# Second attention with softmax numerators turned by VectorE and value products in eight tiles; inverse sums spread by DMA

## The chip, the cores and the metric

The kernel runs on one core of one Trainium2 chip. The core has a matrix engine (TensorE, PE in the rows), whose weight loads have rows of their own (PEld), and four others: VectorE (DVE), ScalarE (ACT), GpSimd (POOL) and SyncE (SP), which issues most DMA transfers. Each engine works through its own queue in order; they wait for each other by semaphores. The metric is the time of one execution in device microseconds (us).

## What is computed

A network of two blocks of two layers each works on 512 tokens of width 1024, all in float32. The layers are: a convolution and state-space mixer with a feed-forward part; the first attention (causal, with forget gates, 16 heads of 64) with a feed-forward part; the second attention (grouped: 16 query heads, 4 key and value heads of 64) with an MLP; a gated MLP over tokens with an MLP. What the change touches is the two attentions. The second one, cut to the core:

```python
q = apply_rope(rmsnorm(q.reshape(B, T, N_HEADS, HEAD_DIM), q_g), cos, sin)
k = apply_rope(rmsnorm(k.reshape(B, T, N_KV_HEADS, HEAD_DIM), k_g), cos, sin)
v = v.reshape(B, T, N_KV_HEADS, HEAD_DIM)
def one_block(q_blk):                      # 128 queries
    s = jnp.einsum('bqkgd,bskd->bkgqs', q_blk, k).astype(jnp.float32) * scale
    p = jax.nn.softmax(s, axis=-1).astype(v.dtype)
    return jnp.einsum('bkgqs,bskd->bqkgd', p, v)
...
return o @ w_o
```

The first attention is the same in form, with 16 key heads, a causal mask and a term from cumulated forget gates added to the scores; it ends in `o @ w_out` too.

## The kernel before, in words

The whole program is one list of stages that every engine runs through in the same order. The dense products take each weight and activation as a sum of a high and a low part and make three matmuls of each product (`whi,ahi`, `wlo,ahi`, `whi,alo`). A weight arrives by SyncE in pieces of 512 KB (`raw`), ScalarE makes the high part and GpSimd the low part (L590, 128x1024), in a ring of buffers. A dense stage is eight such units; `fo` is the product after the first attention, `o` the one after the second.

Both attentions run through one set of functions, `pe_attn`, `act_attn` and `dve_attn`, with A = 0 for the first and A = 1 for the second. The work is cut into 32 groups: group g holds 128 queries (tile g % 4) of a pair of heads (pair g // 4), so 8 pairs in all. For each group:

- TensorE makes the scores of both heads into two PSUM banks (`scores_gqa`, L2638, for the second attention; 64 rows of the array for each head, 256 keys at a time).
- VectorE takes the row maxima (L1784, 128x1024 for both heads), negated, into `rowst`.
- ScalarE takes the exponential (L1028), one head at a time, into `pbuf`, and accumulates the row sums beside it. The sums are not applied yet: `pbuf` holds softmax numerators, P.
- TensorE transposes P in blocks of 128x128 (`transposed`, L2565) into two banks. ScalarE copies one head out to `ptb` (L1016), VectorE the other (L1796).
- TensorE multiplies with the values (`weigh`, L2544): 4 key blocks times two heads, each head on 64 columns of the array, results in bank OBANK with head dimension on partitions and queries along the row.

For each pair VectorE also inverts the row sums (L1801) and copies them out to 64 columns per head (`rdup`, L1805); TensorE transposes `rdup` (`spread`, L2555), so that the inverse stands once for each head dimension; VectorE copies that out of PSUM (`rinv_t`, L1811) and multiplies the value products by it while it takes them to `oT` (`pv_out`, L1814). An fp32 matmul is two instructions in the trace, and each has a weight load.

The order within TensorE's queue is written out by hand in `pe_attn`: scores of two groups, transposes of the group before, then a spread or, in the second attention, the build of a q tile (`pe_build_q`, L2685), then value products of two earlier groups, and transposes again. In the second attention half of q still gets its norm and rope while the loop runs: VectorE sums squares, and GpSimd does 20 steps of rope (`rope_q1`, L610 to L619, `q1_step`), which the q tiles from pair 4 on wait for.

What starts after the loop: `o` waits for `oT` of the pairs that it contracts; its unit j needs the pairs 2j and 2j+1, split into high and low by ScalarE (`ahi`) and VectorE (`alo`, L1552).

Of the kernel before, what the change touches and what calls it, by code (L numbers as in the profile page):

```python
# [22 lines left out]
P = 128  # L23
# [30 lines left out]

SC_B, SC_C, SC_H, ZCOL = 0, D, 2 * D, 3 * D
# [48 lines left out]
KEEP_START = (14, 24)  # L104
SMALL_AFTER, FORGET_AFTER, CUM_AFTER = 3, 8, 11
# [53 lines left out]
def build_in(ctx, nc, a, out):  # L159
# [70 lines left out]
    rowst = take("rowst", [P, 3, 64])  # L230
# [50 lines left out]
    rdup = at("rdup", [P, NT, P], arena_at + 1024 * 84)  # L281
# [18 lines left out]
    ptb2 = scratch("ptb2", [P, TSLOTS, T], 0)  # L300
# [18 lines left out]
    def sem(name):  # L319
# [42 lines left out]
    at_s, at_max, at_exp, at_rinv, at_tp, at_pt_a, at_pt_d, at_pv, at_r, at_o = (  # L362
        sem(n) for n in ("at_scores", "at_max", "at_exp", "at_rinv", "at_tp", "at_pt_act", "at_pt_dve", "at_pv",
                         "at_recip", "at_o"))
    at_rc, at_rv = sem("at_recip_copied"), sem("at_recip_value")
# [168 lines left out]

    def sp_gate_rows(sp, L):
# [10 lines left out]
    def _(sp):  # L546
# [10 lines left out]
        sp_t(sp, "fo", w_fo, 4, [0, HALF])  # L557
# [4 lines left out]
        sp_t(sp, "o", w_o, 4, [0, HALF])  # L562
# [23 lines left out]
    def _(pool):  # L586
# [34 lines left out]

        def lo_spot(u):

            pool.wait_ge(w_hi, u + 1)
            pool.tensor_tensor(spot_lo[u][:], raw[:, u % RING], spot_hi[u][:].bitcast(F32), ALU.subtract).then_inc(w_lo, 1)
# [7 lines left out]
        rope_turn = END["qkv"] // RING  # L633
        assert END["qkv"] % RING == 0
        done = 0
        for turn in sorted({u // RING for u in SPOTTED} | {rope_turn}):
            if turn > done:
                turns(done, turn)
            for j in range(RING):
                u = turn * RING + j  # L640
                if turn == rope_turn and j == RING - 1:
                    rope_q1()
                if u in SPOTTED:
# [360 lines left out]
    def act_attn(act, A, ptb, causal, hook, turn, build=None):  # L1004
# [13 lines left out]
        def exps(g):  # L1018
# [6 lines left out]
            for n in (2 * g, 2 * g + 1):  # L1025
                if n >= PSLOTS:
                    act.wait_ge(at_tp, B + n - PSLOTS + 1)
                act.activation(pbuf[:, n % PSLOTS, 0:N], ps[:, n % 4, 0:N], ACT.Exp, bias=rowst[:, 0, n:n + 1],  # L1028
                               accum_out=rowst[:, 1, n:n + 1]).then_inc(at_exp, 1)

        for n in range(PERIODS):
# [7 lines left out]
            p_out(2 * n)  # L1039

# [125 lines left out]
    def act_build_at(act, g):  # L1166

        p = g // 4 + 1
        if g % 4 == 0 and Q_FIRST <= p < 8:
            act.wait_ge(bd_tp, K_BUILDS + p + 1)  # L1170
            act.activation(qT[:, p], ps[:, RBANK], ACT.Copy, scale=HD ** -0.5).then_inc(bd_ev_a, 1)
# [84 lines left out]
    def gate_head(s):  # L1256

        def head(act, split, step):
            if s == 2:
                act.wait_ge(gm_uv, NGM)  # L1260
            if s == 0:
                act.wait_ge(at_o, 14)
            step(2, 2, 0, 0)
            if s == 0:
                act.wait_ge(at_o, 16)
# [9 lines left out]
    def _(act):  # L1275
# [27 lines left out]
        def beside_fox(g):  # L1303
            if g == 28:
                act.wait_ge(at_o, 4)
# [1524 lines left out]
```

## Time and profile before

| | |
|---|---|
| median of 3 runs | 2753.12 us (2753.07 to 2753.45) |
| the profiled execution, its own time | 2753.73 us |
| its span, first to last instruction | 2751.9 us |
| mean granted TensorE clock | 0.999 |
| busy: PE, DVE, ACT, POOL | 2729.1, 1304.9, 1101.4, 1156.5 us |
| first attention: scores to first product of fo | about 903 to 977.0 us |
| second attention: scores of group 2 to first product of o | 1464.6 to 1569.2 us |

TensorE is busy for 99% of the span. The two attentions are some 180 us of 2752; the dense products are nearly all of the rest. In the rows below times are us from the start of the span; "x16" is a count of instructions, "ns" the mean of one, the last column the idle time before, with the engine, tile and line that ended it. PE's ends are modelled, so start-to-start says more than durations. Instructions of one line that follow each other stand in one row.

### The profile page before, as it was taken

Reading aid. Unit: us, or ns where it says so; the run is one execution under the profiler, and the core shown is the slowest. Engines: PE = TensorE matmul, PEld = TensorE weight load, DVE = VectorE, ACT = ScalarE, POOL = GpSimd, SP = SyncE. Lnnn points to the kernel's source line nnn. Section 1 sums busy time; section 2 is a strip of 40 time slices with the busy share of each in tenths; the row PEclk is TensorE's granted clock in tenths of the full one; section 3 lists DMA queues with packets and bytes.
Section 4 is the critical chain, followed back from the end, with each engine's and each line's share of the span. In section 5 each row is a group of like instructions: output and inputs, shape, how many; then the busy total and the mean of one; then the engine's idle time right before and its main releaser. Section 6 shows DMA issues by size and latency. Waiting matters only on the chain.

```text
span 2751.9 us, 37617 instructions
## 1 busy us (share of the span) xinstructions
PE 2729.1 (99%) x13805; PEld 2260.9 (82%) x13805; DVE 1304.9 (47%) x1545; ACT 1101.4 (40%) x1641; POOL 1156.5 (42%) x472
## 2 busy tenths in 40 slices
PE   9999999999999999999999999999999999999999
PEld 7888888888888888888877888888788888888887
DVE  4157459883351658884477651123424543321232
ACT  4343443333442644334356552334433223432332
POOL 4433445444534035544444044444445334444443
PEclk9999999999999999999999999999999999999999
DMA  6322236863433025863330033333333223333322
GB/s 164 85 77 77 81 96 214 255 195 96 103 93 94 15 85 175 258 215 114 93 97 24 15 95 99 97 101 99 122 104 97 83 77 107 92 96 96 107 92 76
DMA packets 319846, 299.98 MB, mean 109 GB/s; under 512 B 16308, under 2 KB 251256, under 8 KB 319608
## 3 DMA queue, kind: packets, MB, share of 16 engines
q1 hardware_dynamic: 304712, 236.70, 29.6%
q10 hardware_dynamic: 15024, 61.75, 6.6%
q8 instruction: 76, 1.25, 0.2%
q14 instruction: 34, 0.28, 0.0%
HBM read 296.30 MB, written 2.11 MB: 108 GB/s over the span
## 4 chain that ended last, share of the span: by engine, by line
PE 69%; issue 17%; POOL 10%; DVE 3%; ACT 1%; POOLq 0%; DVEq 0%; ACTq 0%
POOL wlo L590 10%; PE ps L2301 10%; PE ps L2302 9%; PE ps L2303 9%; PE ps L2117 9%; PE ps L2118 9%; PE ps L2119 9%; PE ps L2565 2%; PE ps L2544 2%; PE ps L2638 1%; PE ps L2225 1%; PE ps L2227 1%; PE ps L2226 1%; PE ps L2721 1%; PE ps L2622 1%
## 5 line engine op out<-in xcount | busy, mean ns | idle before, releaser
L590 POOL TENSOR_TENSOR wlo<-raw,whi 128x1024 fp32r<-128x1024 f32 x434 | 1107.3, 2556 | 1550.8 <-ACT whi L664 1463.1
L2117 PE MATMUL ps<-xhi,whi 128*128 128x512 f32 x1664 | 653.5, 393 | 1.5 <-POOL wlo L590 1.5
L2119 PE MATMUL ps<-xhi,wlo 128*128 128x512 f32 x1664 | 647.7, 389 | 0.0
L2118 PE MATMUL ps<-xlo,whi 128*128 128x512 f32 x1664 | 647.6, 389 | 0.0
L664 ACT ACTIVATE whi<-raw 128x1024 fp32r<-128x1024 f32 x424 | 444.8, 1052 | 272.1 <-PE ps L2303 142.7
L2301 PE MATMUL ps<-whi,ahi 128*128 128x512 f32 x1168 | 455.2, 390 | 0.7 <-DVE alo L1561 0.7
L2303 PE MATMUL ps<-whi,alo 128*128 128x512 f32 x1168 | 454.4, 389 | 0.0
L2302 PE MATMUL ps<-wlo,ahi 128*128 128x512 f32 x1168 | 454.4, 389 | 0.0
L2117 PEld LDWEIGHTS ps<-xhi,whi 128*128 128x128 f32 x1664 | 312.5, 188 | 68.2 <-POOL wlo L590 2.2
L2119 PEld LDWEIGHTS ps<-xhi,wlo 128*128 128x128 f32 x1664 | 312.4, 188 | 65.6
L2118 PEld LDWEIGHTS ps<-xlo,whi 128*128 128x128 f32 x1664 | 312.5, 188 | 65.0 <-issue 1.4
L2301 PEld LDWEIGHTS ps<-whi,ahi 128*128 128x128 f32 x1168 | 219.2, 188 | 47.3 <-issue 1.0
L2303 PEld LDWEIGHTS ps<-whi,alo 128*128 128x128 f32 x1168 | 219.2, 188 | 45.5
L2302 PEld LDWEIGHTS ps<-wlo,ahi 128*128 128x128 f32 x1168 | 219.3, 188 | 45.1
L1561 DVE TENSOR_TENSOR alo<-hid_mlp,ahi 128x1024 fp32r<-128x1024 f32 x60 | 76.4, 1273 | 242.1 <-ACT ahi L862 242.1
L1957 DVE SCALAR_TENSOR_TENSOR hid_mlp<-ps,relu 128x512 f32 (+1 forms) x64 | 44.3, 692 | 272.9 <-ACT relu L1187 272.9
L2301 PE MATMUL ps<-whi,xhi 128*128 128x512 f32 x416 | 164.3, 395 | 2.3 <-POOL wlo L590 1.3
L1721 DVE SCALAR_TENSOR_TENSOR acc<-adaraw,ccol,acc 128x1536 f32<-128x1536 f32 x60 | 162.3, 2733 | 5.8 <-DMA adaraw<-in_ada_w 5.7
L2303 PE MATMUL ps<-whi,xlo 128*128 128x512 f32 x416 | 162.1, 390 | 0.0
L2302 PE MATMUL ps<-wlo,xhi 128*128 128x512 f32 x416 | 162.0, 389 | 0.0
L862 ACT ACTIVATE ahi<-hid_mlp 128x1024 fp32r (+1 forms) x60 | 63.7, 1062 | 205.2 <-PE ps L2303 205.2
L1187 ACT ACTIVATE relu<-ps 128x512 f32<-128x512 f32 x64 | 38.3, 599 | 225.0 <-PE ps L2119 214.2
(337 smaller groups left out, 3216.1 us busy)
## 6 DMA issues: line engine op xcount, KB each, us to landing
adaraw<-in_ada_w ACTq DMA_DIRECT2D x64, 768.0 KB, 6.1
raw<-in_ffn_w_up SPq DMA_DIRECT2D x88, 512.0 KB, 4.1
raw<-in_mlp_w_in SPq DMA_DIRECT2D x64, 512.0 KB, 4.0
raw<-in_mlp_w_out SPq DMA_DIRECT2D x64, 512.0 KB, 3.7
raw<-in_gmlp_w_in SPq DMA_DIRECT2D x48, 512.0 KB, 3.9
raw<-in_sc_ssm_w_in SPq DMA_DIRECT2D x44, 512.0 KB, 3.8
raw<-in_ffn_w_down SPq DMA_DIRECT2D x44, 512.0 KB, 3.7
raw<-in_fox_w_in SPq DMA_DIRECT2D x24, 512.0 KB, 3.8
```

The source lines that it names most:

```text
L590: pool.tensor_tensor(wlo[:, z], raw[:, j], whi[:, z].bitcast(F32), ALU.subtract).then_inc(w_lo, 1)
L664: act.activation(whi[:, z], raw[:, s], ACT.Copy).then_inc(w_hi, 1)
L862: act.activation(ahi[:, (m0 + j) % 2], x, ACT.Copy).then_inc(a_hi, 1)
L1561: dve.tensor_tensor(alo[:, s], x, ahi[:, s].bitcast(F32), ALU.subtract).then_inc(a_lo, 1)
L1721: dve.scalar_tensor_tensor(x, adaraw[s][:], ccol[:, bass.ds(i * 4 + (m - 4), 1)], x, ALU.mult, ALU.add).then_inc(ada_acc, 1)
L2117: pe.matmul(out, lh, rh, start=start, stop=False)
L2118: pe.matmul(out, lh, rl, start=False, stop=False)
L2119: return pe.matmul(out, ll, rh, start=False, stop=stop)
L2301: pe.matmul(out, lh[:, k, c], wh[:, k], start=st, stop=False, skip_group_check=True)
L2302: pe.matmul(out, lh[:, k, c], wl[:, k], start=False, stop=False, skip_group_check=True)
L2303: ins = pe.matmul(out, ll[:, k, c], wh[:, k], start=False, stop=False, skip_group_check=True)
L2544: ins = pe.matmul(ps[64 * b:64 * b + 64, OBANK, i * P:(i + 1) * P], v_of(2 * pr + b, c), ptb[:, (2 * g + b) % TSLOTS, c * P:(c + 1) * P], ...
```

## The change

1. In the second attention P is no longer transposed by TensorE. VectorE turns it in blocks of 32x32 (`turned`, one instruction of 128x1024 per group, after the maximum of the next group). In the result partition 32r + k holds key k of every block of 32 keys, for the 32 queries of row group r. The numerators stay in `pbuf2`, the turned ones go to `ptb2`, three buffers of one pair each.
2. A value product then contracts over 32 keys: 32 rows by 64 columns of the array. Four row groups (32 queries of each tile each, results in banks 4 to 7) and two column halves (the two heads) are eight tiles. The values must stand in all four row groups: SyncE makes these copies (`sp_v_rep`, 16 transfers, twice).
3. The value products are made in five parts: two pairs at a time for the first six pairs (each part in two halves of 64 matmuls), then one pair at a time (128 matmuls each, 128 columns). `PV_STEPS` says after which scores they stand.
4. ScalarE takes the parts out of PSUM (`out`), and no longer copies `ptb`. q tiles are built at other groups (`BUILD_AT`), into free halves of banks 4 and 5.
5. In both attentions the inverse sums are no longer spread by TensorE. VectorE inverts into a small tile and turns it (128x32); SyncE writes it to DRAM in four pieces and reads it back onto 64 partitions for each head; GpSimd multiplies `oT` in place (`normalise`), ahead of the low part of unit 3 of `fo` or `o`. SyncE's chain of these copies stands before its load of unit 7. ScalarE's splits wait for the normalised pairs.

TensorE in the middle of the second attention. In the rows `consts` is the identity, `kT,qT` are scores, `pbuf` is P, `rdup` are inverse sums, `qr` is q after rope; x counts matmuls. Before:

```order
L2685 MATMUL ps<-consts,qr 128x128 x4
L2544 MATMUL ps<-ptb_157,v_148 64x128 x16
L2565 MATMUL ps<-consts,pbuf 128x128 x8
L2638 MATMUL ps<-kT,qT 128x256 x8
L2565 MATMUL ps<-consts,pbuf 128x128 x8
L2555 MATMUL ps<-consts,rdup 128x128 x4
L2544 MATMUL ps<-ptb_157,v_148 64x128 x16
```

And now, from group 14 to the end of the attention:

```order
L2804 MATMUL ps<-consts,qr 128x128 x4
L2757 MATMUL ps<-kT,qT 128x256 x12
L2804 MATMUL ps<-consts,qr 128x128 x4
L2757 MATMUL ps<-kT,qT 128x256 x8
L2835 MATMUL ps<-ptb_158,vrep_161 64x256 x64
L2757 MATMUL ps<-kT,qT 128x256 x4
L2835 MATMUL ps<-ptb_158,vrep_161 64x256 x64
...
L2757 MATMUL ps<-kT,qT 128x256 x12
L2835 MATMUL ps<-ptb_158,vrep_162 64x128 x256
L2433 MATMUL ps<-whi,ahi 128x512
```

The transposes and spreads are gone, and the value products, which stood after every two groups, stand in blocks, one group of scores between two halves, and the last two parts in one block before the first product of `o`.

VectorE over one pair in the same place. Before:

```order
L1784 TENSOR_REDUCE rowst<-ps 128x2 x2
L1796 COPY ptb_157<-ps 128x512
L1811 COPY rinv_t<-ps 128x512
L1814 TENSOR_TENSOR oT_144<-ps,rinv_t 128x512
L1796 COPY ptb_157<-ps 128x512
L1784 TENSOR_REDUCE rowst<-ps 128x2 x2
L1796 COPY ptb_157<-ps 128x512
L1801 RECIPROCAL rowst<-rowst 128x8
L1805 COPY rdup<-rowst 128x512
L1796 COPY ptb_157<-ps 128x512
```

And now:

```order
L1889 TENSOR_REDUCE rowst<-ps 128x2
L1904 STREAM_TRANSPOSE ptb_158<-pbuf_159 128x1024
L1889 TENSOR_REDUCE rowst<-ps 128x2
L1904 STREAM_TRANSPOSE ptb_158<-pbuf_159 128x1024
L1889 TENSOR_REDUCE rowst<-ps 128x2
L1904 STREAM_TRANSPOSE ptb_158<-pbuf_159 128x1024
L1889 TENSOR_REDUCE rowst<-ps 128x2
L1904 STREAM_TRANSPOSE ptb_158<-pbuf_159 128x1024
L1875 RECIPROCAL rinv<-rowst 128x4x2
L1880 STREAM_TRANSPOSE rcol<-rinv 128x32
```

The copies out of PSUM are gone, and each maximum is followed by the block transpose of the group before it.

GpSimd at the end of rope, where the low parts of `o` begin. Before:

```order
L616 TENSOR_TENSOR rb<-qn,gcs 128x256 x2
L619 TENSOR_TENSOR qr<-ra,rb 128x512
L590 TENSOR_TENSOR wlo<-raw,whi 128x1024
```

And now:

```order
L672 TENSOR_TENSOR rb<-qn,gcs 128x256 x2
L675 TENSOR_TENSOR qr<-ra,rb 128x512
L684 TENSOR_TENSOR oT_145<-oT_145,rinv_160 128x512 x8
L646 TENSOR_TENSOR wlo<-raw,whi 128x1024
```

The eight multiplications, one for each pair, stand between rope and the low part of unit 3.

The core of the diff (q builds, renamed semaphores and the memory layout left out):

```diff
+PV_PARTS = ((0, 1), (3, 2), (4, 5), (6,), (7,))
+PV_STEPS = {11: (0, 0, 8), 12: (0, 8, 16), 19: (1, 0, 8), 20: (1, 8, 16), 27: (2, 0, 8), 28: (2, 8, 16), 31: (3, 0, 16)}
+PV_OUT = {12: 0, 20: 1, 28: 2}
+BUILD_AT = {5: 2, 9: 3, 14: 4, 17: 5, 22: 6, 25: 7}
...
+    def sp_spread(sp, A):
+        spread = rinv2 if A else rinv_t
+        for m in range(8 * A, 8 * A + 8):
+            if m == 10:
+                sp_v_rep(sp, 1)
+            rows = inv_rows[m].rearrange("b (t q) -> (b t) q", q=P)
+            sp.wait_ge(at_rt, m + 1)
+            for i in range(NT):
+                sp.dma_start(rows[:, 32 * i:32 * i + 32], rcol[32 * i:32 * i + 8]).then_inc(at_rw, 16)
+            sp.wait_ge(at_rw, 64 * (m + 1))
+            if m:
+                sp.wait_ge(at_n, m)
+            for b in range(2):
+                sp.dma_start(spread[64 * b:64 * b + 64], inv_rows[m][b:b + 1].to_broadcast([64, T])).then_inc(at_rr, 16)
...
+        def normalise(A, oT, spread):
+            for pr in range(8):
+                m = 8 * A + pr
+                pool.wait_ge(at_o, m + 1)
+                pool.wait_ge(at_rr, 32 * (m + 1))
+                pool.tensor_tensor(oT[:, pr], oT[:, pr], spread[:], ALU.mult).then_inc(at_n, 1)
...
+        def turned(g):
+            pr, i = divmod(g, 4)
+            dve.wait_ge(at_exp, 64 + 2 * g + 2)
+            if pr == 2:
+                dve.wait_ge(q_sum, 14) if i < 2 else dve.wait_ge(q1_step, Q1_STEPS)
+            if pr in (3, 4):
+                dve.wait_ge(at_pvp, 1)
+            if pr in (5, 6):
+                dve.wait_ge(at_pvp, 2)
+            if pr == 7:
+                dve.wait_ge(at_pvp, 3)
+            dve.transpose(ptb2[:, pr % 3, i].rearrange("p b n -> p (b n)"), pbuf2[:, g % 2].rearrange("p b n -> p (b n)")
+                          ).then_inc(at_turn, 1)
+            if i == 3:
+                dve_inverse(dve, 1, pr)
...
-        def spread(pr):
-            pe.wait_ge(at_rinv, 8 * A + pr + 1)
...
-            for i in range(NT):
-                q = QT[i] if causal else i
-                ins = pe.transpose(ps[:, RBANK, q * P:(q + 1) * P], rdup[:, i], ident)
-            ins.then_inc(at_r, 1)
...
+    def pe_gqa(pe):
+        def weigh(i, first, end):
+            pairs = PV_PARTS[i]
...
+            if first == 0:
+                pe.wait_ge(at_turn, 4 * max(pairs) + 4)
...
+            N = len(pairs) * P
+            for j in range(first, end):
+                for r in range(4):
+                    rows = slice(32 * r, 32 * r + 32)
+                    for b in range(2):
+                        ins = pe.matmul(ps[64 * b:64 * b + 64, 4 + r, 0:N], vrep[kv // 2][rows, j, kv % 2],
+                                        ptb2[rows, b0:bufs[-1] + 1:step, :, b, 32 * j:32 * j + 32],
+                                        start=j == 0, stop=j == 15)
...
+        for g in range(2, 32):
+            pe.wait_ge(at_exp, 64 + 2 * g - 2)
+            scores_gqa(pe, g).then_inc(at_s, 1)
+            if g in BUILD_AT:
+                pe_build_at(pe, BUILD_AT[g])
+            if g in PV_STEPS:
+                weigh(*PV_STEPS[g])
+        weigh(4, 0, 16)
```

## Rows read from the trace of the kernel before

**Rows 1.** Busy time by stretch, second attention: stretch, length, busy time (instructions), clock, DMA

```profile
core 0: us, PE busy (x) PEld busy (x) DVE busy (x) ACT busy (x) POOL busy (x), PEclk, DMA share, GB/s
1520.00:1540.00 20.00, 20.00 (x216) 16.93 (x213) 15.12 (x20) 12.39 (x32) 0.00 (x0) 1.00 0.01 2
```

**Rows 2.** Chain that ended last, 1464 to 1570, shares by line

```profile
by line: PE ps L2565 27.3%; PE ps L2638 26.2%; PE ps L2544 25.2%; POOL sqb L604 3.8%; PE ps L2555 3.5%; DVE rowst L1784 3.1%; PE ps L2685 2.5%; DVE alo L1552 2.2%; DVE ptb L1796 1.8%; DVE q1raw L2090 1.2%; PE ps L2303 0.7%; DVE hsum L1947 0
```

**Rows 3.** Timeline of PE, one period of the second attention: start, duration, instructions

```profile
1540.54 1.97 PE L2544 MATMUL ps<-ptb,v 128*64 128x128 f32 x32
1542.44 1.09 PE L2565 MATMUL ps<-consts,pbuf 128*128 128x128 f32 x8
1543.46 2.00 PE L2638 MATMUL ps<-kT,qT 64*128 64x256 f32 x16
...
1546.32 0.60 PE L2555 MATMUL ps<-consts,rdup 128*128 128x128 f32 x4
1546.85 1.97 PE L2544 MATMUL ps<-ptb,v 128*64 128x128 f32 x32
```

**Rows 4.** Busy time by stretch, first attention, columns as in the first group

```profile
923.00:941.00 18.00, 17.93 (x210) 14.92 (x208) 13.27 (x24) 11.32 (x41) 0.00 (x0) 1.00 0.01 2
```

**Rows 5.** Timeline of PE in the first attention: a spread, what follows, the last spread

```profile
913.20 0.60 PE L2555 MATMUL ps<-consts,rdup 128*128 128x128 f32 x4
913.73 1.53 PE L2544 MATMUL ps<-ptb,vtok 128*64 128x128 f32 x24
...
974.98 0.66 PE L2555 MATMUL ps<-consts,rdup 128*128 128x128 f32 x4 [0.35 <-DVE rdup L1805]
```

**Rows 6.** Timeline of POOL in the fo product: one low part of a weight unit

```profile
990.33 2.48 POOL L590 TENSOR_TENSOR wlo<-raw,whi 128x1024 fp32r<-128x1024 f32 x1 [2.96 <-ACT whi L664]
```

**Rows 7.** DMA issues of the whole span: count, KB each, median us from issue to landing

```profile
consts<-in_consts SPq DMA_DIRECT2D x1, 64.0 KB, 2.1
...
gate_rows<-modc SPq DMA_DIRECT2D x4, 4.0 KB, 12.0
```

**Rows 8.** Groups of DVE instructions, 1464 to 1569.3: count, busy us, mean ns

```profile
L1784 DVE TENSOR_REDUCE rowst<-ps 128x2 f32<-128x1024 f32 x30 | 35.6, 1219 | 6.4 <-PE ps L2638 6.3
L1796 DVE COPY ptb<-ps 128x512 f32<-128x512 f32 x32 | 22.0, 686 | 13.6 <-PE ps L2565 13.6
...
L1552 DVE TENSOR_TENSOR alo<-oT,ahi 128x1024 fp32r<-128x1024 f32 x2 | 2.4, 1219 | 0.0
L1801 DVE RECIPROCAL rowst<-rowst 128x8 f32<-128x8 f32 x8 | 1.5, 192 | 0.0
```

**Rows 9.** Timeline of DVE: the maximum of group 5, and two back to back

```profile
1476.98 1.22 DVE L1784 TENSOR_REDUCE rowst<-ps 128x2 f32<-128x1024 f32 x1
...
1500.48 2.35 DVE L1784 TENSOR_REDUCE rowst<-ps 128x2 f32<-128x1024 f32 x2 [0.38 <-PE ps L2638]
```

**Rows 10.** Groups of ACT instructions, 1464 to 1569.3: the exponentials

```profile
L1028 ACT ACTIVATE pbuf<-ps,rowst 128x512 f32<-128x512 f32 x62 | 42.1, 690 | 29.0 <-DVE rowst L1784 29.0
...
L1028 ACT ACTIVATION_READ_ACCUMULATOR pbuf<-ps,rowst 128x1 f32 x62 | 12.8, 206 | 0.0
```

**Rows 11.** Timeline of POOL: the last step of rope

```profile
1497.75 1.28 POOL L619 TENSOR_TENSOR qr<-ra,rb 128x512 f32<-128x512 f32 x1
```

**Rows 12.** Timeline of PE at the end of the second attention, and the start of o

```profile
1562.17 1.09 PE L2565 MATMUL ps<-consts,pbuf 128*128 128x128 f32 x8
1563.19 1.09 PE L2544 MATMUL ps<-ptb,v 128*64 128x128 f32 x16
1564.21 1.09 PE L2565 MATMUL ps<-consts,pbuf 128*128 128x128 f32 x8
...
1569.22 0.50 PE L2301 MATMUL ps<-whi,ahi 128*128 128x512 f32 x1
```

**Rows 13.** PE alone by stretch, early second attention: busy time (instructions), granted clock, DMA

```profile
1469.80:1473.20 3.40, 1.53 (x18) 1.00 0.00 0
1473.25:1476.60 3.35, 3.35 (x18) 0.50 0.00 0
```

## What is forecast

> **What bounds the kernel now.** I read the second attention first, since nearly all of the change is there, and in it the table of busy time by stretch: between 1520 and 1540 us TensorE is busy for 20.00 of 20 us, VectorE for 15.12 and ScalarE for 12.39 [rows 1]. The chain that ended last says the same by line: 82.2% of it there is TensorE's own transposes (L2565), scores (L2638), value products (L2544) and spreads (L2555) [rows 2]. The timeline gives the period: value products start at 1540.54 and again two groups later at 1546.85, so two groups take 6.31 us: products 1.90, transposes some 1.0 twice (the second row is left out), scores 1.93, and a spread 0.53, or a q build in its place [rows 3]. Nothing waits, so whatever leaves TensorE here is gained until another engine is late, and VectorE is next. The first attention is bound in the same way: TensorE 17.93 of 18 us, VectorE 13.27 [rows 4].
>
> **Part 1: first attention, spreads gone.** A spread begins at 913.20 and the next work at 913.73: 0.53 us, and there are 8 [rows 5], so 4.2 us; the last waited 0.35 us besides, for VectorE. VectorE gives up two copies per pair and gets one small transpose, so it doesn't become the bound. The sums now go to DRAM and back, and GpSimd multiplies. The last multiplication may be late, but only the part of the fo product that uses the last pairs needs it: a unit lasts 2.48 + 2.96 = 5.44 us [rows 6], and the fourth begins 16.3 us after the first. The multiplication stands on GpSimd ahead of the low weight part of fo's fourth unit (2.48), and SyncE's load of unit 7 stands behind the whole chain of copies; both have that 16 us and more as cover. The copies' price is bounded by small transfers: 2.1 us for 64 KB and 12.0 for 4 KB [rows 7]. Twice 2.1 plus 1.3, 1.1 and 1.2 for multiplication and split is under 8 us, hidden; twice 12.0 would be some 28, and would cost about 11 in each attention. The 12.0 us is one set of four rows written while other stages load, so I take 2.1 and count the other in the range only in part. Term: -4.0 (-4.6 to -3).
>
> **Part 2: second attention, what a group costs.** TensorE loses per two groups both transposes and the spread. VectorE's two copies per two groups (686 ns each [rows 8]) become two 32x32 block transposes of 128x1024. That operation isn't in the trace. The nearest row of its size between the same memories is L1552 (1219 ns); two maxima of 128x1024 take 2.35 us where one lasts 1.22, so back to back such an operation costs 1.13 to 1.14 [rows 8, 9]. I take 1.18 for a transpose, with 1.14 and 2.44 (twice the row) as ends. Per group VectorE then has 1.14 + 1.18 + a quarter of an inverse (0.19 for the reciprocal and about as much for a small transpose, say 0.35) = 2.4 us. ScalarE has two exponentials at most 2 x (0.69 + 0.21) = 1.8 [rows 10], TensorE 0.97 of scores. So VectorE becomes the bound, at 2.4 in place of 3.16 a group.
>
> **Part 3: where it waits.** The transpose of group 10 waits for the end of GpSimd's rope, at 1497.75 + 1.28 = 1499.03 [rows 11]. That chain doesn't change, and it is the anchor. VectorE at 2.4 a group from the maximum of group 5, at 1477 [rows 9], has turned group 9 by 1491, and has then only one maximum to do until 1499. So the sum can start at 1499, and what TensorE does in this hole is free: the two halves of part 0.
>
> **Part 4: the products' price.** A half of a double part is 64 products, 128 instructions of 256 columns (each fp32 product is two). Scores of 256 columns in two row halves: 16 instructions in 1.93, that is 8 steps of two at 0.24 [rows 3]; if all eight tiles (four row groups, two column halves) run together, a half is 16 steps, 3.5 to 3.9; I take 3.6. A single part is 256 instructions of 128 columns; by 32 in 1.90, 16 steps of two [rows 3], it is 32 steps or 3.8, but then an instruction has to come every 15 ns, and the shortest spacing that a row shows is 59 ns (1.90/32), where width and not supply sets it. Bounds 3.8 and 15.1; I take 5.5, near the lower end, since those 59 ns say nothing against a faster supply.
>
> The Trainium skill, page "TensorEngine Tiling (Array Packing)", section "Instruction Overhead", gives a matmul about 60 cycles however short it is. At 2.4 GHz that is an estimate of 25 ns, so 6.4 us for a single part and no limit on the halves; the sum would be 1.8 us higher. No row here shows an instruction that short.
>
> **Part 5: the sum.** From 1499.0: 22 transposes x 1.18 = 26.0, 20 maxima x 1.14 = 22.8, six inverses 2.1, together 50.9. Parts 1 and 2 each put two halves between scores: scores then come 0.97 + 3.6 apart while VectorE has 2.4 of work and some 0.4 in hand, a stall of 1.8, four times 7.2. The end: after the scores of group 31 TensorE does parts 3 and 4, 11.0; VectorE needs about 4.9 of that to its last transpose; so 6.1 after it, and 0.3 for the first product of o. 1499.0 + 50.9 + 7.2 + 6.4 = 1563.5, where o begins at 1569.22 before [rows 12]: -5.7. ScalarE's copies out of PSUM lie beside VectorE's work; SyncE's 16 replicating copies ahead of the third pair may hold back the write that an inverse waits for, 0 to 4, which I leave to the range.
>
> One thing is added: TensorE now idles more than half of each period. From 1469.80 to 1473.20 it was busy 1.53 of 3.40 us, and in the next 3.35 us its granted clock was 0.50, the 1.2 GHz level of the two [rows 13]. Scores at that level take twice 0.97, still under 2.4; a half of a part would stall VectorE by up to 3.6 more. I take +2.0, about one half so struck and another in part, with 0 and +6 as ends. Second attention -3.7, first -4.0: -7.7. Against the median, which is 0.6 below the profiled execution, 2753.1 - 7.7 = **2745.4**. Own range of this case: all lower ends (single parts 3.8, transposes 1.14, no clock loss) give about -14, the upper ends (single parts 8, clock +6) about +3: 2739 to 2756.
>
> **The rivals.** *Fewer tiles at a time, the slower side.* No row shows more than two products at once: sixteen value products on two column halves take 1563.19 to 1564.21, just as long as eight transposes on one tile before them, 1562.17 to 1563.19 [rows 12]. That eight steps suffice for sixteen, though both passes of one product stand next to each other, says that the second tile doesn't wait for the first one's second pass; it speaks for overlap of more, but doesn't show it. With four at a time a half is 7.2 and a single part 7.6: stalls 4 x 5.4 = 21.6, part 0 reaches some 6 past the hole, the end is 10.6: 1499.0 + 6 + 50.9 + 21.6 + 10.6 = 1588, +19, with the first attention +15: 2768. Each us on a half costs about 7.8 in all, so the case decides from a half of 4.6 us on, which is 6.3 tiles at a time.
>
> *Two at a time.* Then TensorE is the bound from 1491 on: 20 scores 19.4, six halves of 13.6, two singles of 14.1, four q builds 2: 131, ending at 1622, +53 and -4: 2802. The Trainium skill, page "TensorE: Matmul & The Clock Gate", section "What overlaps and what doesn't", says that matmuls start and end strictly in program order. By that rule, with both passes of a product next to each other, only a last pass and the next first pass overlap, and this is the time; the sixteen in eight steps above speak against it (it would be nine).
>
> *A block transpose at half the rate* (2.44): VectorE needs 28 more from 1499, part 0 starts 7 later and loses its hole, stalls shrink by 5: about +16 for the attention and +12 in all: 2765.
>
> *The clock eats it.* If the clock is at 1.2 GHz for most halves and both single parts, the second attention loses about 10 rather than 2, and only the first one's gain stands, against which +4 is set: 2753, no change.
>
> **How the numbers follow.** Likeliest case 0.56, four at a time 0.14, two at a time 0.09, slow transpose 0.06, clock 0.12, copies through DRAM that come late (up to +11 for each attention) 0.03. Under about 0.2% (5.5 us) a difference can't be told from none: faster is below 2747.6. The likeliest case lies there by about 0.8, else mostly within 0.2%: faster 0.46, same 0.21, slower 0.33. The range must reach the cases above until 0.2 is left out: it runs from 2739 to 2775 and leaves out two at a time, late copies and the ends.
>
> **What would show it.** In the changed kernel's timeline: first attention shorter by 4 with no spread and no new idle time; block transposes of 1.14 to 1.22; maxima 2.4 apart in the steady stretches; a half of a double part in 3.5 to 3.9 and a single part under 6.5; VectorE idle from about 1492 to 1499 for rope; o's first product about 1560 to 1564 less 4. A half of 7 or 14 us, or a clock at 0.5 in most stretches after 1500, would prove me wrong; so would GpSimd's multiplications holding up unit 3 of fo or o.

## The result, and the profile after

The changed kernel takes 2758.71 us (median of 17 runs) where the kernel before takes 2753.92 (17 runs): 1.0019 times as long, with a 95% interval of 1.0013 to 1.0026. The forecast was 2745.4, 7.7 us faster; it came out 4.8 us slower. The profiled execution took 2761.48 us, 2.8 above the median, with a span of 2759.6, so the pieces read in this trace add up to more than 4.8. Its product fo begins at 977.56 (977.02 before) and o at 1576.76 (1569.22 before [rows 12]); so the first attention lost 0.9 us (the trace was 0.4 us ahead of the old one when it began) and the second 7.0.

The largest single piece is one stop of VectorE. Its timeline in the changed kernel (start, duration, instructions, idle time before and what ended it), first at the wait for rope, then 13 us later:

```profile
1493.43 1.18 DVE L1889 TENSOR_REDUCE rowst<-ps 128x2 f32<-128x1024 f32 x1
1499.48 1.25 DVE L1904 STREAM_TRANSPOSE ptb<-pbuf 128x1024 f32<-128x1024 f32 x1 [4.87 <-POOL qr L675]
1500.65 1.19 DVE L1889 TENSOR_REDUCE rowst<-ps 128x2 f32<-128x1024 f32 x1
1501.76 1.22 DVE L1904 STREAM_TRANSPOSE ptb<-pbuf 128x1024 f32<-128x1024 f32 x1
1502.91 0.16 DVE L1875 RECIPROCAL rinv<-rowst 128x8 f32<-128x8 f32 x1
...
1512.35 0.16 DVE L1875 RECIPROCAL rinv<-rowst 128x8 f32<-128x8 f32 x1
1519.13 0.21 DVE L1880 STREAM_TRANSPOSE rcol<-rinv 128x32 f32<-128x32 f32 x1 [6.63 <-DMA inv_rows<-rcol]
1519.27 1.18 DVE L1889 TENSOR_REDUCE rowst<-ps 128x2 f32<-128x1024 f32 x1
```

Maxima and block transposes run back to back, 1.11 and 1.15 us each from start to start. Then the small transpose for pair 3 waits 6.63 us until the write of pair 2's inverses has landed, because both use the tile `rcol`. The queue of SyncE, which issues that write, tells why it is late (start, time over which the issues were spread, transfers):

```profile
1505.24 1.09 SPq L588 DMA_DIRECT2D rinv<-inv_rows  x2
1506.37 10.30 SPq L572 DMA_DIRECT2D vrep<-v  x16
1516.72 1.50 SPq L583 DMA_DIRECT2D inv_rows<-rcol  x4
```

Sixteen copies of V take 10.3 us to issue, 0.64 each, and the write that VectorE needs stands behind them. They also began late. The copies themselves wait only for the end of rope (1499.38), but the read of pair 1's inverses (L588), which stands in front of them, waited for GpSimd's normalisation of pair 0. SyncE's queue from 1500 to 1520 (who waited for whom: us in total, times, longest):

```profile
SPq L586 <- POOL oT L684: 14.9, 1, 14.9
```

TensorE's timeline shows what it cost there, what a half of a part costs, and the end of the attention:

```profile
1497.40 3.71 PE L2835 MATMUL ps<-ptb,vrep 32*64 32x256 f32 x128
1501.04 1.13 PE L2757 MATMUL ps<-kT,qT 64*128 64x256 f32 x8
...
1521.98 2.08 PE L2757 MATMUL ps<-kT,qT 64*128 64x256 f32 x8 [7.20 <-ACT pbuf L1125]
1523.99 5.35 PE L2835 MATMUL ps<-ptb,vrep 32*64 32x256 f32 x128
1529.27 1.13 PE L2757 MATMUL ps<-kT,qT 64*128 64x256 f32 x8
...
1563.30 3.22 PE L2835 MATMUL ps<-ptb,vrep 32*64 32x128 f32 x150
1567.20 1.82 PE L2835 MATMUL ps<-ptb,vrep 32*64 32x128 f32 x106 [0.69 <-issue]
1569.81 0.65 PE L2835 MATMUL ps<-ptb,vrep 32*64 32x128 f32 x21 [0.78 <-ACT oT L1115]
1571.15 3.33 PE L2835 MATMUL ps<-ptb,vrep 32*64 32x128 f32 x128 [0.69 <-issue]
1574.88 1.96 PE L2835 MATMUL ps<-ptb,vrep 32*64 32x128 f32 x107 [0.40 <-issue]
1576.76 0.51 PE L2433 MATMUL ps<-whi,ahi 128*128 128x512 f32 x1
```

A half is 1501.04 - 1497.40 = 3.64 us. That is all eight tiles together: in the trace the instructions start in eights, 0.216 us apart, and this is what TensorE has in work just before a next start (1498.09 to 1498.10):

```profile
1497.88 0.42 PE L2835 MATMUL ps<-ptb,vrep 32*64 32x256 f32 x8
```

The half after the stop took 5.28: by stretch (length, busy time with instructions, granted clock, DMA) the clock was down there.

```profile
1512.00:1522.00 10.00, 2.80 (x18) 0.67 0.33 86
1522.00:1524.00 2.00, 2.00 (x10) 0.50 0.05 11
1524.00:1529.30 5.30, 5.30 (x132) 0.68 0.00 0
1529.40:1534.00 4.60, 4.60 (x138) 1.00 0.03 7
```

At the end two single parts cover 1563.30 to 1576.76, 13.5 us where I had 11.0. In the first attention the spreads are gone, but TensorE now waits once in each pair, and at the end 2.45 us where it waited 1.37 before (at 966.66 in that trace):

```profile
912.91 1.53 PE L2676 MATMUL ps<-ptb,vtok 128*64 128x128 f32 x24
914.92 1.06 PE L2687 MATMUL ps<-consts,pbuf 128*128 128x128 f32 x8 [0.47 <-ACT ptb L1082]
...
922.01 1.53 PE L2676 MATMUL ps<-ptb,vtok 128*64 128x128 f32 x24
...
967.38 0.30 PE L2687 MATMUL ps<-consts,pbuf 128*128 128x128 f32 x1 [2.45 <-DVE ptb L1942]
```

The period is 922.01 - 912.91 = 9.10 us; before, spreads stood 9.09 apart (913.20 [rows 5] and 922.29). The 0.53 us of a spread came back as a wait of 0.47.

### The profile page after: what moved, and what is told of

Its sections match the earlier page's. It is cut to its first block, busy times and chain, and to the rows that moved or that the text cites. A ratio compares the mean times of both kernels' runs of the same rounds, so it can differ in the third digit from the quotient of the medians.

```text
span 2759.6 us, 38508 instructions
## 1 busy us (share of the span) xinstructions
PE 2706.1 (98%) x14253; PEld 2231.8 (81%) x14253; DVE 1306.4 (47%) x1522; ACT 1091.0 (40%) x1617; POOL 1185.0 (43%) x488
## 3 DMA queue, kind: packets, MB, share of 16 engines
q8 instruction: 78, 1.28, 0.2%
## 4 chain that ended last, share of the span: by engine, by line
PE 67%; issue 18%; POOL 11%; DVE 3%; ACT 1%; SPq 0%; DMA 0%; POOLq 0%; DVEq 0%; ACTq 0%
POOL wlo L646 10%; PE ps L2433 9%; PE ps L2435 9%; PE ps L2434 9%; PE ps L2249 9%; PE ps L2250 9%; PE ps L2251 9%; PE ps L2835 1%; PE ps L2357 1%; PE ps L2359 1%; PE ps L2358 1%; PE ps L2874 1%; PE ps L2687 1%; PE ps L2741 1%; PE ps L2254 1%
```

## The experiments

The theory after the first look: the stop of VectorE behind SyncE's sixteen issues is most of the loss; the first attention was never bound by TensorE; the sum for the second attention was otherwise right.

**Copies of V later.** One line moves:

```diff
-            if m == 10:
-                sp_v_rep(sp, 1)
             rows = inv_rows[m].rearrange("b (t q) -> (b t) q", q=P)
             sp.wait_ge(at_rt, m + 1)
             for i in range(NT):
                 sp.dma_start(rows[:, 32 * i:32 * i + 32], rcol[32 * i:32 * i + 8]).then_inc(at_rw, 16)
+            if m == 11:
+                sp_v_rep(sp, 1)
             sp.wait_ge(at_rw, 64 * (m + 1))
```

> The changed kernel with one edit on SyncE: the second set of 16 copies of V is issued after the write of pair 3's inverses instead of before the write of pair 2's. Theory (queue on SyncE): the 16 issues take 10.3 us on SyncE, pair 2's write stands behind them, and VectorE's inverse of pair 3 waits 6.6 us for that write; with the edit this wait goes, VectorE's gap before the maximum of group 16 falls under 0.5 us, and the kernel is 6 to 7 us faster than the changed one, 2752. Rival (the wait only covers another that ends next, rope's end or the part of value products): the gap moves to the next wait and less than 2 us is gained, 2757.

Measured: 2749.41 us (11 runs), 0.9987 of before (0.9978 to 0.9996), and 9.3 us below the changed kernel by medians (9.0 when each is taken against the kernel before that was measured beside it). VectorE in its trace:

```profile
1510.48 0.21 DVE L1880 STREAM_TRANSPOSE rcol<-rinv 128x32 f32<-128x32 f32 x1
1510.62 1.18 DVE L1889 TENSOR_REDUCE rowst<-ps 128x2 f32<-128x1024 f32 x1
```

And SyncE, where the sixteen issues now stand in time in which it had nothing else to do:

```profile
1510.72 1.56 SPq L581 DMA_DIRECT2D inv_rows<-rcol  x4
1512.32 12.55 SPq L572 DMA_DIRECT2D vrep<-v  x16
1524.97 1.18 SPq L588 DMA_DIRECT2D rinv<-inv_rows  x2
```

The wait is gone and no other took its place. The gain is larger than the wait of 6.6: the half that ran at a lower clock behind the stop (5.28) is 3.64 again, and the two single parts take 12.8 us at a clock of 1.00, where they took 13.5 at 0.80. So the order in SyncE's queue alone made the difference between slower and faster than before.

**First attention as before.** The spreads, the two copies and the multiplication by VectorE come back for A = 0, and SyncE's and GpSimd's part of it goes:

```diff
+        def spread(pr):
+            pe.wait_ge(at_rinv1, pr + 1)
+            for i in range(NT):
+                ins = pe.transpose(ps[:, RBANK, i * P:(i + 1) * P], rdup[:, i], ident)
+            ins.then_inc(at_r1, 1)
...
-        sp_t_between(sp, "fo", w_fo, [0, HALF], lambda: sp_spread(sp, 0))
+        sp_t(sp, "fo", w_fo, 4, [0, HALF])
```

> The changed kernel with the first attention as before (spreads by TensorE, VectorE applies the inverse), the second attention as changed. Theory (the first attention is bound by a loop of score, maximum, exponential and copy of one period's length, in which the spread was free, and it lost at its end by VectorE's split running beside GpSimd's multiplication): fo begins 0.9 us earlier than in the changed kernel, so about 2757.8, and TensorE's wait of 0.47 for ScalarE's copy in each pair is gone. Rival, the step of the prediction (each spread cost 0.5 us, lost again only by the end): fo begins 2 to 4 us later, 2761 to 2763.

Measured: 2760.14 us (9 runs), 1.4 above the changed kernel. By medians, then, the change of the first attention is worth 1.4 us, neither my theory's loss of 0.9 nor the forecast's gain of 4. The size is uncertain: the intervals of the two against the kernel before overlap (1.0013 to 1.0026 and 1.0018 to 1.0038). The traces say why there is no one number: against the kernel before, and from the first attention's start, fo begins 0.9 later in the changed kernel, 1.1 earlier in the one with the copies later (same code there), and within 0.1 in this one. Seven traces of runs with that same code (also those of the experiments below that leave the first attention alone) show 80.95 to 84.26 us from its start to fo; before it was 82.07. What differs is the end. There VectorE's two splits stand ahead of a copy that TensorE waits for, and GpSimd's multiplication may run beside them. VectorE and GpSimd in the changed kernel:

```profile
962.60 3.44 DVE L1645 TENSOR_TENSOR alo<-oT,ahi 128x1024 fp32r<-128x1024 f32 x2
```

```profile
963.23 1.73 POOL L684 TENSOR_TENSOR oT<-oT,rinv_t 128x512 f32<-128x512 f32 x1 [9.57 <-DMA rinv_t<-inv_rows]
```

And in the kernel with the copies later, where GpSimd starts 0.6 us later:

```profile
962.58 2.36 DVE L1645 TENSOR_TENSOR alo<-oT,ahi 128x1024 fp32r<-128x1024 f32 x2
```

```profile
963.81 2.25 POOL L684 TENSOR_TENSOR oT<-oT,rinv_t 128x512 f32<-128x512 f32 x1 [10.13 <-DMA rinv_t<-inv_rows]
```

Alone a split takes 1.2 and the multiplication 1.28. The lengths fit the two taking turns: a multiplication that begins within the first split (three of the seven traces) holds up the second, 3.44 in all, and one that begins within the second split (two traces) waits itself, 2.25 and 2.31. So 0.6 us in the landing of the read that the multiplication waits for decides it. TensorE waits 2.45 in the one and 1.4 in the other, and of these two only the longer wait is followed by a lower clock, by stretch from 968 to 972: 0.62 and 1.00. (After waits of 1.50 and 1.68, in two of the other traces, it was 0.70 and 0.74.)

```profile
968.00:972.00 4.00, 4.00 (x30) 0.62 0.16 38
```

```profile
968.00:972.00 4.00, 3.53 (x46) 1.00 0.21 66
```

(the changed kernel first, then the one with the copies later).

**Copy first in the first attention.** To test whether a loop over the engines sets its period, with the copies of V later:

```diff
-            exps(2 * n)
             p_out(2 * n - 1)
+            exps(2 * n)
             exps(2 * n + 1)
```

> The kernel with the copies of V later, and in the first attention ScalarE copies the transposed P of group 2n-1 out of PSUM before the exponentials of group 2n instead of after them. Theory (the first attention's period of 9.1 us is a loop over the engines in which that copy stands behind two exponentials; the spread's 0.5 us was free in it): TensorE's wait of 0.47 per pair for that copy goes, the period falls to 8.7 or less, and fo begins 2.5 to 3.5 us earlier than without the edit. Rival (the exponentials, now later, set the period): no gain, or later.

Measured: the wait of 0.47 is gone and the period is 8.58 us. TensorE:

```profile
912.39 0.83 PE L2687 MATMUL ps<-consts,pbuf 128*128 128x128 f32 x6
...
920.97 0.82 PE L2687 MATMUL ps<-consts,pbuf 128*128 128x128 f32 x6
```

So the loop was right. But the time is 2749.36 (11 runs), no change: at the end TensorE waited 2.1 us for VectorE's copy and 1.9, in two, for exponentials, the clock was 0.77 from 960 to 968 and 0.61 from 968 to 972, and in this trace fo began about 1 us later, counted from the attention's start, than without the edit. The gain of the middle was lost at the end.

**The end of the first attention.** The same, with ScalarE's split in two pieces and VectorE's in four between other work:

```diff
-            if g == 28:
-                act.wait_ge(at_n, 4)
-                act_first_splits(act, oT1)
+            if g in (24, 28):
+                act.wait_ge(at_n, 2 if g == 24 else 4)
+                act_first_splits(act, oT1, ((g - 24) // 4,))
...
-            if g == 29:
-                dve_first_splits(dve, "fo", oT1)
+            if g in (25, 27, 29, 31):
+                m, k = divmod((g - 25) // 2, 2)
+                dve.wait_ge(a_hi, A0["fo"] + m + 1)
+                ins = dve.tensor_tensor(alo[:, m, k], oT1[:, 2 * m + k], ahi[:, m, k].bitcast(F32), ALU.subtract)
```

> Copies of V later, ScalarE's copy first in the first attention, and VectorE's two splits of the first attention's result cut into four pieces of 128x512, one each before the maxima of groups 25, 27, 29 and 31. Theory (the end of the first attention loses what its middle gains: the splits hold up VectorE's copy, TensorE idles for some 2 us, and the clock then falls to 0.5): no wait over 1 us at that end, granted clock 1.00 to fo, fo begins 3 us earlier than in the kernel with only the copies of V later, 2746. Rival (the end waits for something else): fo within 1 us of it, 2749.

Measured: 2749.35 us (11 runs). In the trace the longest wait is 1.34, the clock 1.00 from 960 on, and fo begins 2.2 us earlier than before from the attention's start, 1.1 more than with the copies later alone. The medians don't show it: the runs lie between 2747.4 and 2751.4, and what differs between them isn't settled.

**Rope earlier.** The root on ScalarE and the reciprocal on VectorE move up one group, with the copies of V later:

```diff
-            if g == 4:
+            if g == 3:
                 act_q1_std(act)
...
-            if g == 5:
+            if g == 4:
                 dve_q1_rstd(dve)
```

> The kernel with the copies of V later, and the root and the reciprocal of the second half of q's norm one group earlier on ScalarE and VectorE. Theory (the second attention hangs on the end of rope, the anchor of the prediction's sum; VectorE waits 4.8 us for it): rope starts 2 to 2.8 us earlier and o begins as much earlier, 2747. Rival (the exponentials of group 3, which then stand behind ScalarE's table loads, cost as much): no gain.

Measured: 2748.04 us (11 runs), 1.4 less, but the intervals against the kernel before overlap (0.9972 to 0.9990, and 0.9978 to 0.9996 without the edit). Rope ended 2.6 us earlier against the attention's start, but part 0 then ended last: its halves ran from 1493.55 to 1502.77 in this trace, the first one partly at a lower clock (0.76 from 1493 to 1498). The trace is of the slowest of the 11 runs, 4.6 us above their median, and its second attention is no shorter than without the edit, so the gain of the median isn't seen in it.

**All of them.** Rope earlier, the copy first, and the splits of both engines at two places:

```diff
-            if g == 29:
-                dve_first_splits(dve, "fo", oT1)
+            if g in (25, 29):
+                dve_first_splits(dve, "fo", oT1, ((g - 25) // 4,))
```

> Copies of V later, ScalarE's copy first in the first attention, rope earlier, and the splits of the first attention's result done one at group 24 and 25 and one at group 28 and 29 instead of both at 28 and 29. Theory: the gains add, about 3 in the first attention, 1 to 2 at its end (VectorE's two splits hold up TensorE by 1.4 to 2.5 us, and GpSimd's multiplication beside them makes one longer), 2 to 2.8 from rope: 2742 to 2744. Rival (each is hidden by the next wait): 2748 or more.

Measured: 2749.39 us (11 runs): the rival. At the end of the first attention TensorE still waited 3.7 us in two, the clock was 0.57 from 968 to 972, and fo began 2.9 later, counted from the attention's start, than with the copies of V later alone. With VectorE's splits in four pieces instead, as in the run on the end of the first attention:

> The same with rope one group earlier. Theory: 1 us more, as rope alone gave 1.4 (the halves of part 0 then end last, no longer rope): 2745. Rival: nothing more.

Measured: 2746.00 us (9 runs), 0.9974 of before (0.9964 to 0.9984). It is the fastest of all kernels here by its median, 7.4 us below the kernel before and 12.7 below the changed one, and all nine runs (2748.41 at most) lie below all eleven with the copies later alone (2748.72 at least).

**The last two pairs together.** 256 columns, 256 instructions, after the last transpose:

```diff
-PV_PARTS = ((0, 1), (3, 2), (4, 5), (6,), (7,))
+PV_PARTS = ((0, 1), (3, 2), (4, 5), (6, 7))
```

> The changed kernel with the last two pairs as one double part (256 columns, 256 instructions) after the last block transpose, in place of two single parts (128 columns, 512 instructions). Theory (a single part is set by the supply of instructions, 22 ns each and gaps, and part 4 also waits for ScalarE's copy of part 3): two halves of 3.6 us begin at the last transpose's end, 7.3 us or less of supply gaps in place of 9.4 from that end to the first product of o: 1.5 to 2 us faster, 2757. Rival (columns set the time): the same columns in all, but part 3 no longer runs ahead of the last transpose, so 1 to 2 us slower, 2760.

Measured: 2759.13 us (11 runs), as the changed kernel within its noise. TensorE at the end:

```profile
1566.17 9.58 PE L2834 MATMUL ps<-ptb,vrep 32*64 32x256 f32 x256 [4.19 <-DVE ptb L1903]
1575.68 0.50 PE L2432 MATMUL ps<-whi,ahi 128*128 128x512 f32 x1
```

No gap of supply is left, but the 256 took 9.5 instead of 7.3 us after 4.19 us of idling; the clock was 0.50 from 1566.2 to 1570 and 0.90 from there on. The run doesn't tell supply from columns; what the single parts lose to supply was given back by a slower start.

**TensorE kept busy.** Four products of the identity after the scores of most groups, which nothing reads, with the copies of V later:

```diff
             scores_gqa(pe, g).then_inc(at_s, 1)
+            if g not in PV_STEPS and g not in (13, 21, 29):
...
+                for _ in range(4):
+                    pe.matmul(ps[:, 6, 256:384], ident[:], ident[:], start=False, stop=True, skip_group_check=True)
```

> As the one with the copies of V later, and with four products of the identity (eight instructions, 0.87 us) after the scores of each group without value products, except the group after a part's end; they write where nothing is read, and only keep TensorE busy. Theory (clock): the granted clock stays at 1.00 over the second attention from group 10 on, where it was 0.5 in several stretches; gained are 1.5 to 3 us against the kernel without filling. Rival (scores at half clock are hidden under VectorE, only a half of value products so struck counts, and the filling delays what follows it): no gain or up to 2 us lost.

Measured: 2751.75 us (11 runs), 2.3 more than without. The granted clock was 1.00 from 1462 to 1500 and from 1520 on, 0.91 between, where it had been 0.74 to 1.00 by stretch; still the second attention took 1.6 us longer in its trace (1.9 less than before, not 3.5). That is what the rival said: scores at half clock hidden under VectorE, and a filling that delays what comes after it. What the clock costs by itself the run doesn't tell, since the filling takes TensorE's time as well.

**How many tiles run together.** The same products in another order, with the copies of V later: first one row group through all key blocks of a half, then the next.

```diff
-            for j in range(first, end):
-                for r in range(4):
-                    rows = slice(32 * r, 32 * r + 32)
+            for r in range(4):
+                rows = slice(32 * r, 32 * r + 32)
+                for j in range(first, end):
```

> The kernel with the copies of V later, and the same value products in another order: one row group's products over all its key blocks, then the next row group's, so that neighbours in the queue share a row group and only the two column halves alternate. Theory (TensorE starts products of other tiles past a waiting one, but only those near in its queue): two at a time, a half takes 13.5 to 14 us in place of 3.7, and the kernel is 55 to 75 us slower. Rival (the queue looks far enough ahead to find all four row groups): a half stays near 3.7.

Measured: 2897.36 us (one run), 148 more. A half took about 20 us, and the clock was at 0.50 although TensorE was never idle:

```profile
1490.69 19.78 PE L2835 MATMUL ps<-ptb,vrep 32*64 32x256 f32 x128
...
1512.41 22.65 PE L2835 MATMUL ps<-ptb,vrep 32*64 32x256 f32 x128
```

```profile
1500.00:1510.00 10.00, 10.00 (x60) 0.50 0.00 0
```

A step of 256 columns lasts 0.21 us at full clock (8 steps in 1.7 to 1.9 with what stands around them, [rows 3]) and so 0.43 at half. The second half above ran at half clock throughout (0.50 from 1512.4 to 1535): 22.65 / 0.43 is 53 steps for 128 instructions, 2.4 at a time. In the trace they start in twos, 0.427 us apart, and four run together only around the three changes of row group. Just before a next start (1513.71 to 1513.74):

```profile
1513.31 0.64 PE L2835 MATMUL ps<-ptb,vrep 32*64 32x256 f32 x2
```

At full clock two at a time would be 64 x 0.21 = 13.6 us, as the rival had it. Two row groups side by side, the other two behind them:

```diff
-            for j in range(first, end):
-                for r in range(4):
-                    rows = slice(32 * r, 32 * r + 32)
+            for h, j, r in ((h, j, r) for h in range(2) for j in range(first, end) for r in (2 * h, 2 * h + 1)):
+                rows = slice(32 * r, 32 * r + 32)
```

> Copies of V later, and the value products in an order in which neighbours in the queue belong to two row groups and two column halves, the other two row groups following after a half's key blocks. Theory (TensorE takes what is near in its queue): four at a time, a half of 7 to 7.4 us at full clock; with one row group at a time two ran together and the granted clock was 0.5, so here I expect the clock between: 0.5 to 1. By the prediction's rival 19 us more than all eight at full clock, 2768; at half clock throughout some 60 more. Rival (the queue finds all row groups): 3.7 and no loss.

```profile
1491.60 6.35 PE L2835 MATMUL ps<-ptb,vrep 32*64 32x256 f32 x128
...
1567.28 13.08 PE L2835 MATMUL ps<-ptb,vrep 32*64 32x128 f32 x256
1581.17 13.16 PE L2835 MATMUL ps<-ptb,vrep 32*64 32x128 f32 x256 [0.81 <-ACT oT L1115]
```

Measured: 2780.77 us (one run), 31 more than with all row groups side by side. A half takes 6.3 us at a clock of 1.00; the two single parts, with the clock at 0.54 from 1565 to 1592, took 26 together. Just before a next start (1492.28 to 1492.30):

```profile
1492.08 0.39 PE L2835 MATMUL ps<-ptb,vrep 32*64 32x256 f32 x4
```

So what runs together is what stands near in the queue: eight, four and two tiles, by the order alone.

## Why the prediction was wrong

The forecast was -7.7, the result +4.8: 12.5 us apart. Copies of V later takes 9.3 of them away; the first attention, -4.0 forecast and -1.4 by medians, is 2.6; 0.6 is left, less than these medians can tell. The result lies inside the range that the forecast gave, but the range was that wide for fewer tiles at a time, a slow transpose and the clock, and none of these is what cost most of the time.

- **The step that failed** is in part 5: the sixteen copies ahead of the third pair, "0 to 4, which I leave to the range". Moving them alone gave 9.3. I bounded when a transfer lands and never counted what sixteen issues take of SyncE itself, though each has to pass before the write behind it. Issued at 0.64 each they are 10.3 us, begun only when the normalisation of pair 0 let the read of pair 1 before them go (1505.24): a wait of 14.9 us in the same queue that I had not placed either. With that count the term would have been in the sum and not in the range, and the forecast would have been slower.
- **Part 1 was wrong in its step from "nothing waits" to "whatever leaves TensorE is gained".** TensorE was busy 17.93 of 18 us [rows 4], but its work hid a loop of the same length: scores, maximum, two exponentials, copy, transposes. The spread lay in the slack of that loop. The edit of the copy's place, which took the period from 9.10 to 8.58, shows it.
- **Part 2 held.** A block transpose takes 1.15 us (1.18 forecast), a group 2.26 and with the inverse 2.4.
- **Part 3 held.** Rope ends at 1499.38 (1499.03), and VectorE waits for it 4.87 us. The halves of part 0 (1492.70 to 1501.04) outlast that hole, but VectorE waits for nothing behind them.
- **Part 4 held for the halves** (3.64, 3.6 forecast) and was low for the single parts: 5.7 and 6.95 us against 5.5, and part 4 begins 0.8 late because it writes where ScalarE still reads part 3. The rows of the end show gaps of 0.40 to 0.69 us that no semaphore explains ("issue"), and the granted clock was 0.86 from 1563.3 to 1569 and 0.75 from 1570 on. The Trainium skill's 60 cycles per matmul ("TensorEngine Tiling (Array Packing)", section "Instruction Overhead"), an estimate of 25 ns, is what 128 instructions in 3.33 us come to (26 ns). In the kernel with the copies later 128 came in 2.08 us between longer gaps, 16 ns each, so the trace doesn't bear it out as a floor; as a mean it comes near, since both parts with all gaps and waits are 512 instructions in 12.8 us, 25 ns each.
- **The sum** for the second attention, without the stop, was -3.7; the kernel with the copies of V later shows -3.5 in its trace (o begins 5.0 earlier than before, fo 1.5). That it fits so well is partly luck: the +2.0 for the clock was meant for a half at half clock, and there all six halves took 3.64; in its place the end behind the last block transpose took 8.2 us (6.4 forecast), and VectorE's waits behind the halves and the q builds were 8.2 (7.2 forecast).
- **The clock** did fall as feared (0.50 from 1522 to 1524). Where it met value products it cost 1.6 us in the half behind the stop and about 0.7 in the single parts. What it costs at the end of the first attention isn't told apart from the wait ahead of it, and the filling doesn't show what it costs elsewhere.
- **The rivals.** All eight tiles did run together. Four at a time by order cost 31 (one run) and not 19: its single parts took 26.2 us near half clock, about twice what four at a time would take at full clock, so by this estimate 13 of the 31 are the clock's. Two at a time cost 148 (one run) where I had 53: its halves took 18 to 23 us (13.6 forecast) and its single parts 24 and 25 (14.1), at a clock of 0.50 to 0.63. The 7.8 us that I gave for each us on a half doesn't follow from my own case of four, where the end moves by 24.6 for 3.6, or 6.8. The rule of the Trainium skill that matmuls start strictly in program order ("TensorE: Matmul & The Clock Gate", section "What overlaps and what doesn't") doesn't hold for these products: 128 with both passes next to each other took 3.64 us and started in eights, where that rule, as the prediction read it, allows two at a time. The slow transpose didn't come. What came was the mechanism that I had priced last, and with a range instead of a count.

## What to carry to other kernels

Before a transfer is put into an engine's queue, count the issues that it takes (here 0.64 us each), look at what the queue already waits for ahead of them (here 14.9 us), and name the first instruction behind them and who waits for it; an issue that nobody needs for 30 us belongs behind one that is needed next. An engine that never waits isn't yet the bound: follow one buffer around the engines and compare that loop with the period before counting a removed instruction as gained. Small tiles on TensorE paid here only where neighbours in its queue lay on different tiles.

## What was not expected of the hardware

- The issue of one transfer of 32 x 4 x 128 took 0.64 us of SyncE's queue, 10.3 us for sixteen; with the copies later the sixteen took 12.55.
- The opening says that each engine works through its queue in order. TensorE's value products didn't start in that order: although the two instructions of a product stand next to each other, eight, four or two started together, by how many different tiles stood near each other (steps of 0.216 us for 256 columns at full clock).
- The granted clock fell to 0.50 while TensorE was never idle, when only one row group of 32 rows and two column halves worked at a time; with two row groups it was 1.00 for products of 256 columns and near 0.5 for those of 128; with all four it was 1.00 in the halves of the changed kernel that began without a long stop before them (1492.70, 1497.40, 1530.33).
- VectorE's two splits took 3.44 us instead of 2.36 when GpSimd's multiplication ran beside them, and the multiplication up to 2.31 instead of 1.28; which of the two is longer goes with which began first, in all seven traces with that code: begun before the splits the multiplication took 1.3, within the first split 1.42 to 1.73 (and the splits 3.44), within the second 2.25 and 2.31 (and the splits 2.36).
